# One core: both halves of one modulation vector summed on VectorE, several mixer steps handed to ScalarE and GpSimd, and one routing reorder

## The chip, the cores and the metric

One core of a Trainium2 chip. The metric is the device time of the program in microseconds (us); smaller is better. The kernel before has a median of 685.8 us over 3 runs (685.34 to 686.16). The trace that is read below is one further, profiled execution of it.

## The reference

A trunk of two layers over 256 tokens of width 1024, in float32. Every sub-layer is an RMS norm that is shifted, scaled and gated by vectors computed from the conditioning input c; a layer is a mixer (layer 0: sparse attention beside a spatial gating unit; layer 1: pooling) and then a mixture of 32 experts.

```python
cs = jax.nn.silu(c)
for i in range(DEPTH):
    mod = cs @ w_mod[i] + b_mod[i]                      # 1024 x 6144 per layer
    sh_m, sc_m, g_m, sh_f, sc_f, g_f = jnp.split(mod, 6, axis=-1)
    h = modulate(rmsnorm(x, norm_mix[i]), sh_m, sc_m)
    y = hybrid_ab(h, ...) if i % 2 == 0 else multiscale_pool(h, ...)
    x = x + g_m[:, None, :] * y
    h = modulate(rmsnorm(x, norm_ffn[i]), sh_f, sc_f)
    x = x + g_f[:, None, :] * hier_moe(h, ...)          # router, top 2 of 8 in the top group
return rmsnorm(x, norm_out)

# in hybrid_ab, layer 0:  h @ w_in gives q, kv, q_idx, k_idx, w_idx, u, v
#   attention over the 64 best keys of each query, distance penalty -slope * |i - j|, softmax
#   spatial gating: gelu(u) * (masked(w_s) @ layernorm(gelu(v)) + b_s)
#   concat([attention, gating]) @ w_o
```

## The kernel before, in words

All weights stream once from HBM (268 MB read), on SyncE's DMA queue. Large tiles of 2 MiB ("chunks") land in a few places: four ring slots, and the rooms `scratch` (ATT), `early_w`, `ARENA_A` and `ARENA_B`. The table `front` (L175 on) lists the chunks in their loading order, each with its place; SyncE issues a chunk once the chunk that held the place before has been used up (`slot_freed`), so a late user holds back a transfer and every one behind it in the queue. Later, in the expert loop, each pair of experts takes three transfers of 2 MiB (gate, up, down); the loads of the third pair wait for TensorE's gate matmuls of the first (`gate_next`, L346).

A modulation vector is named (layer, v): v = 0, 1, 2 are the mixer's shift, scale and gate, v = 3, 4, 5 those of the experts. The chunks m4a and m4b are the two halves of (0,4), m3a and m3b of (0,3), n1a and n1b of (1,1), n4a and n4b of (1,4). A half is multiplied by `cs` in one of two ways. TensorE does it in `vector` (L593, 16 matmuls written as 32 records). VectorE does it in `accumulate` (L1438, L1440): four steps over 128x1024, each adding one weight row per partition times a scalar; `reduce` (L614) then sums over partitions on TensorE. The lists `by_pe` and `by_dve` say which chunk goes which way, in order of use.

Each engine's order is written out by hand. In layer 0's mixer they are, around the change:

- VectorE: the index scores, `select(0)` and `select(1)` (best 64 keys), `|dist|` (L1532), `shift` and `divide` of the softmax, then `gelu_v` (polynomial L1514, L1515; after ScalarE's tanh L1539; layernorm statistics L1541 to L1543; GpSimd's power L520; L1546; scaling L1548), `keep_heads(0)` (L1581), the second half of (0,4), the gating unit's bias (L1592), the first half of (0,3), the polynomial of u, `keep_heads(1)`, two products (L1600, L1603, which raises `bT_ready`), the second half of (0,3), the second half of (1,4), and then both halves of (0,5) between the four parts of the residual (L1452, L1453).
- TensorE: scores (L727), the transposes of w_s (L743), q (L680), attention logits, v (L764), transposes of the probabilities (L789), first half of (0,4) (L593), `values(0)` (L797), half of u (L774), w_s times v (L821), second half of u (L774), `values(1)` (L797), the output projection (L841, 64 records), and in its middle the reductions of (0,4) and (0,3).
- ScalarE copies out of PSUM: half of the heads in `keep_heads` (L1217, to catT in `xn`), the tanh of v (L1222) and of u (L1226).
- Layer 0's routing on TensorE: logits (L876, L884), first half of (1,1), first half of (1,4) (both L593), the experts' totals (L902 on, which wait for VectorE's assignment L1667), second half of (1,1), the gather of tokens (L925), the first pair of experts (L960 gate, L972 up).

## Time and profile before

| | |
|---|---|
| median of 3 runs | 685.8 us |
| profiled execution | 686.04 us, of which span 684.3 us |
| TensorE matmul busy | 624.7 us (91%) |
| VectorE, ScalarE, GpSimd busy | 358.2, 179.4, 61.9 us (52, 26, 9%) |
| SyncE's DMA queue | 96.9% of 16 DMA engines' span, 268.22 MB |
| granted TensorE clock | 0.997 of full speed |

The page shows one execution. Busy shares are averages over unlike stages, so they do not say what ends a stage; the timeline of an engine and what ended its idle time do. Every start in a timeline counts from the start of the span. TensorE's float32 matmuls appear as two records each. A released wait is shown in square brackets behind the instruction.

### The profile page before, as it was taken

To read this page: it belongs to the slowest core of one execution; us is meant where nothing else is said; L and a number is where in the kernel's file an instruction comes from. 1 tells how busy PE (TensorE), PEld (TensorE's weight loads), DVE (VectorE), ACT (ScalarE), POOL (GpSimd) and SP (SyncE) were. 2 spreads that over 40 slices of the span, in tenths; PEclk is the share of its full clock that TensorE was granted. 3 is DMA by queue.
4 is the path that set the end of the run, shared out by engine and by line. 5 is a ranking of instruction groups with operands and counts; after the bars stand their busy time and mean duration, and the time that the engine had idled before them with its cause. 6 is when DMAs were issued, how large, how long until landed. Compare 5 with 4: busy or idle time off the path is not lost.

```text
span 684.3 us, 11444 instructions
## 1 busy us (share of the span) xinstructions
PE 624.7 (91%) x4226; PEld 376.5 (55%) x4226; DVE 358.2 (52%) x869; ACT 179.4 (26%) x370; POOL 61.9 (9%) x107
## 2 busy tenths in 40 slices
PE   2699999998999999999998989999999999999894
PEld 1487758446766555545554447676645554555442
DVE  2248988997554643344433464745344334433446
ACT  2123252013431222122311233343122212221213
POOL 5100508930000000000000000000000000000000
PEclk9999999999999999999999999999999999999998
DMA  8999987999899999999999999999999999999991
GB/s 330 355 394 394 370 278 264 404 416 416 352 413 419 420 421 422 420 422 422 422 423 421 409 398 411 422 419 420 421 421 421 422 422 421 422 421 422 422 396 72
DMA packets 51534, 269.63 MB, mean 394 GB/s; under 512 B 4112, under 2 KB 6224, under 8 KB 27440
## 3 DMA queue, kind: packets, MB, share of 16 engines
q1 hardware_dynamic: 50720, 268.22, 96.9%
q0 software_dynamic: 784, 1.01, 0.5%
q8 instruction: 19, 0.31, 0.2%
q14 instruction: 11, 0.09, 0.0%
HBM read 268.17 MB, written 1.05 MB: 393 GB/s over the span
## 4 chain that ended last, share of the span: by engine, by line
PE 69%; DMA 15%; DVE 10%; SPq 2%; issue 1%; ACT 1%; POOL 0%; DVEq 0%; POOLq 0%
PE bank L960 15%; PE bank L972 15%; PE bank L993 13%; PE bank L1019 8%; DMA ring<-in_w_gate 7%; DMA ring<-in_w_mod 4%; PE bank L680 4%; DMA early_w<-in_w_in 3%; DVE gates L1440 3%; PE bank L925 2%; PE bank L764 2%; DVE hT L1758 2%; PE bank L593 2%; PE bank L980 1%; PE bank L1076 1%
## 5 line engine op out<-in xcount | busy, mean ns | idle before, releaser
L960 PE MATMUL bank<-ring,arena 128*64 128x256 f32 x1024 | 116.8, 380 | 2.7 <-DMA ring<-in_w_gate 2.7
L972 PE MATMUL bank<-ring,arena 128*64 128x256 f32 x1024 | 117.2, 381 | 0.0
L960 PEld LDWEIGHTS bank<-ring,arena 128*64 128x64 f32 x1024 | 75.3, 137 | 51.0 <-issue 20.4
L972 PEld LDWEIGHTS bank<-ring,arena 128*64 128x64 f32 x1024 | 72.3, 137 | 41.1 <-issue 8.6
L1758 DVE SCALAR_TENSOR_TENSOR hT<-hT,bank 128x256 f32<-128x256 f32 x32 | 19.2, 601 | 136.6 <-PE bank L972 136.6
L1287 ACT CAST xn_parts<-arena 128x512 fp32r<-128x512 f32 x64 | 39.6, 619 | 106.8 <-DVE arena L1783 106.8
L1783 DVE SCALAR_TENSOR_TENSOR arena<-bank,hT,gates 128x512 f32<-128x512 f32 x64 | 48.0, 750 | 36.7 <-PE bank L993 35.4
L1019 PE MATMUL bank<-xn_parts,sel 128*128 128x512 f32 x256 | 67.0, 405 | 0.0
L993 PE MATMUL bank<-dn_w,hT 128*64 128x512 f32 x256 | 58.5, 598 | 1.1 <-ACT gates L1097 1.1
L1019 PEld LDWEIGHTS bank<-xn_parts,sel 128*128 128x128 f32 x256 | 45.7, 188 | 20.9 <-issue 12.4
L993 PE MATMUL bank<-xn,arena 128*64 128x512 f32 x112 | 51.1, 598 | 0.0
L993 PE MATMUL bank<-gates,arena 128*64 128x512 f32 x112 | 51.1, 598 | 0.0
L1753 DVE SCALAR_TENSOR_TENSOR hT<-hT,bank 128x256 f32<-128x256 f32 x32 | 13.5, 421 | 63.1 <-ACT hT L1274 63.0
L1788 DVE TENSOR_TENSOR xn_parts<-arena,xn_parts 128x512 fp32r<-128x512 f32 x64 | 44.0, 687 | 2.8
L1267 ACT COPY arena<-arena 128x512 f32 x64 | 39.9, 623 | 9.6 <-issue 6.1
L993 PEld LDWEIGHTS bank<-dn_w,hT 128*64 128x64 f32 x256 | 17.4, 136 | 30.9 <-issue 30.9
L593 PE MATMUL bank<-ring,cs 128*32 128x256 f32 x288 | 19.2, 414 | 16.2 <-DMA ring<-in_w_mod 16.2
L1440 DVE SCALAR_TENSOR_TENSOR gates<-ring,cs,gates 128x1024 f32<-128x1024 f32 x23 | 30.1, 1307 | 3.9 <-DMA ring<-in_w_mod 3.2
L980 PE MATMUL bank<-ident,hT 128*128 128x128 f32 x64 | 13.7, 295 | 19.3 <-DVE hT L1758 19.3
L1278 ACT COPY hT<-bank 128x256 f32<-128x256 f32 x16 | 6.0, 372 | 92.6 <-PE bank L980 92.6
L1278 ACT COPY arena<-bank 128x256 f32<-128x256 f32 x16 | 6.0, 373 | 88.1 <-PE bank L980 88.1
L993 PEld LDWEIGHTS bank<-xn,arena 128*64 128x64 f32 x112 | 14.2, 136 | 26.3 <-issue 26.3
(322 smaller groups left out, 761.8 us busy)
## 6 DMA issues: line engine op xcount, KB each, us to landing
ring<-in_w_gate SPq DMA_DIRECT2D x32, 2048.0 KB, 17.2
ring<-in_w_up SPq DMA_DIRECT2D x32, 2048.0 KB, 18.4
ring<-in_w_mod SPq DMA_DIRECT2D x20, 2048.0 KB, 18.4
dn_w<-in_w_down SPq DMA_DIRECT2D x16, 2048.0 KB, 18.2
xn<-in_w_down SPq DMA_DIRECT2D x14, 1024.0 KB, 16.9
gates<-in_w_down SPq DMA_DIRECT2D x14, 1024.0 KB, 19.2
ring<-in_w_in SPq DMA_DIRECT2D x2, 2048.0 KB, 23.8
dn_w<-in_w_mod SPq DMA_DIRECT2D x2, 2048.0 KB, 12.1
```

Of the source, the lines that this page charges most:

```text
L593: ins = pe.matmul(quadrant(vec, q), cs[:, 2, k:k + 1].to_broadcast([P, 32]), by_quadrant(w[:, kk, :], q, natural), start=not last and kk = ...
L680: ins = pe.matmul(bank[banks[m // 2]][:, (m % 2) * T:(m % 2 + 1) * T], w[:, k, m * P:(m + 1) * P], hT[:, k, :], start=(k == 0), stop=(k == ...
L960: ins = pe.matmul(bank[2][h * WIN:(h + 1) * WIN, 0:FE], xw[:, b, h, k, :], w[:, h, 0, k, :], start=(k == 0), stop=(k == KT - 1))
L972: ins = pe.matmul(bank[3][h * WIN:(h + 1) * WIN, 0:FE], xw[:, b, h, k, :], w[:, h, 1, k, :], start=(k == 0), stop=(k == KT - 1))
L993: ins = pe.matmul(bank[n][h * WIN:(h + 1) * WIN, :], actT[b][:, t, h * WIN:(h + 1) * WIN], w[h][:, t, n * HALF:(n + 1) * HALF], start=(t = ...
L1019: ins = pe.matmul(bank[4 + 2 * n + t][:, :], sel[:, b, t * P:(t + 1) * P], xn_parts[:, part, b, n * HALF:(n + 1) * HALF], start=(isinstanc ...
L1267: ins = act.copy(xw[:, b, h], xgT[:, :, bass.ds(start, WIN)])
L1287: act.copy(xn_parts[:, 0, b, at], y_s[:, b, at]).then_inc(e["y_hi"], 1)
L1440: ins = stt(acc, w, cs[:, 2, k:k + 1], acc, ALU.mult, ALU.add)
L1758: stt(act_s.rearrange("s t p -> s p t"), gl.rearrange("s (p t) -> s p t", t=FT), 0.5, bank[3][:, 0:FE].rearrange("s (p t) -> s p t", t=FT) ...
L1783: stt(y_s[:, b, at], bank[n][:, :], slot_gate[:, b:b + 1], gates[:, 2 * l + 1, at], ALU.mult, ALU.mult).then_inc(e["y_kept"], 1)
L1788: tt(xn_parts[:, 1, b, at], y_s[:, b, at], xn_parts[:, 0, b, at].bitcast(F32), ALU.subtract).then_inc(e["y_lo"], 1)
```

## The change

(0,4) moves whole to VectorE: its first half is summed right behind the last `divide`, ahead of `gelu_v`, and starts the sum (one tensor_scalar and three further steps); its second half is then four steps instead of one and three. TensorE's matmuls for m4a go. The reduction of (0,4) now starts the output projection, that of (0,3) stands ahead of the projection's second half.

VectorE gives up: `|dist|`, made by three GpSimd instructions over 128x512 early in the program; the zeroing of a corner of wsT, now a GpSimd memset; the first instruction of both gelu polynomials (0.044715 goes into the scale of ScalarE's square, the 1 into the one VectorE instruction that is left); both copies of `keep_heads`, now two 64-partition copies on ScalarE that both wait for the second half of the values; and the two scaling instructions of the layernorm of v, now two ScalarE instructions with a bias that VectorE prepares in one small one. The transposes of w_s go ahead of the scores on TensorE, into bank 1, and ScalarE copies them in two pieces ahead of the scores' relus. In layer 0's routing, both halves of (1,1) stand ahead of the totals, and the first half of (1,4) behind them.

ScalarE's order from the copy of the transposed probabilities to the one ahead of the squares: L1217, which writes catT (`xn`), is `keep_heads`; the instruction to dn_w of 128x1024 is a tanh. Before:

```order
L1209 COPY arena<-bank 128x512 x2
L1222 ACTIVATE dn_w<-dn_w 128x1024
L1217 COPY xn<-bank 64x4x128
L1105 COPY stage<-bank 128x256
L1191 COPY arena<-bank 128x512
L1192 ACTIVATE dn_w<-bank 128x512
L1212 COPY arena<-bank 128x2x256 x4
L1191 COPY arena<-bank 128x512
L1192 ACTIVATE dn_w<-bank 128x512
L1217 COPY xn<-bank 64x4x128
L1226 ACTIVATE dn_w<-dn_w 128x1024
```

And in the change:

```order
L1213 COPY arena<-bank 128x512 x2
L1228 ACTIVATE dn_w<-dn_w 128x1024
L1223 COPY xn<-bank 64x4x128 x2
L1106 COPY stage<-bank 128x256
L1232 ACTIVATE arena<-arena,stat 128x512 x2
L1195 COPY arena<-bank 128x512
L1196 ACTIVATE dn_w<-bank 128x512
L1216 COPY arena<-bank 128x2x256 x4
L1195 COPY arena<-bank 128x512
L1196 ACTIVATE dn_w<-bank 128x512
L1223 COPY xn<-bank 64x4x128 x2
L1237 ACTIVATE dn_w<-dn_w 128x1024
```

The heads' copies are pairs now, and the layernorm's scaling (L1232) stands ahead of the copies of u. The tanh of u still stands behind the heads' copies.

TensorE's order in layer 0's routing, from the logits to the gather (ARENA_A and ARENA_B are the `arena` rows, ATT is `dn_w`). Before:

```order
L876 MATMUL bank<-hT,wroute 64x256 x8
L884 MATMUL bank<-join,stage 128x40 x2
L593 MATMUL bank<-arena,cs 32x256 x16
L593 MATMUL bank<-dn_w,cs 32x256 x16
L902 MATMUL bank<-ones,rt 32x128
...
L913 MATMUL bank<-rt,ones 128x32
L593 MATMUL bank<-arena,cs 32x256 x16
L925 MATMUL bank<-sel,xn_parts 128x512 x32
```

And in the change:

```order
L879 MATMUL bank<-hT,wroute 64x256 x8
L887 MATMUL bank<-join,stage 128x40 x2
L597 MATMUL bank<-arena,cs 32x256 x32
L903 MATMUL bank<-ones,rt 32x128
...
L914 MATMUL bank<-rt,ones 128x32
L597 MATMUL bank<-dn_w,cs 32x256 x16
L926 MATMUL bank<-sel,xn_parts 128x512 x32
```

The 16 matmuls that read n4a (dn_w) moved from ahead of the totals to behind them.

```diff
-        by_dve = [m2a, m2b, m4b, m3a, m3b, n4b, m5a, m5b]
+        by_dve = [m2a, m2b, m4a, m4b, m3a, m3b, n4b, m5a, m5b]
...
             for t in range(TT):
                 done(pool.iota(dist[:, t, :], [[-1, T]], base=t * P, channel_multiplier=1,
                                allow_small_or_imprecise_dtypes=True))
+            pool.tensor_scalar(keep, dist, -1.0, 0.0, ALU.mult, ALU.max)
+            done(pool.tensor_scalar(dist, dist, 0.0, None, ALU.max))
+            done(pool.tensor_tensor(dist, dist, keep, ALU.add))
+            done(pool.memset(wsT[CHUNK:P, :, 0:CHUNK], 0.0))
...
+            pe.wait_ge(S["small_in"], 16 * SMALL)
+            pe.wait_ge(S["consts"], 2)
+            pe.wait_ge(S["col_turned"], 2)
+            for g in range(4):
+                ins = pe.transpose(bank[1][:, g * P:(g + 1) * P], ws_raw[:, g, :], ident[:])
+            ins.then_inc(S["ws_turned"], 1)
             pe.wait_ge(S["kiT_ready"], 1)
             pe.wait_ge(S["qi_kept"], 2)
...
             turn_p(1)
-            vector((0, 4), (0,))
             pe.wait_ge(S["v_kept"], 2)
...
             values(1)
-            pe.wait_ge(S["cat_act"], 2)
-            pe.wait_ge(S["cat_dve"], 2)
+            reduce((0, 4))
+            pe.wait_ge(S["cat_act"], 4)
             pe.wait_ge(S["u_kept"], 2)
...
-                    if half == 1 and (part, t) == (0, 1):
-                        reduce((0, 4)), reduce((0, 3))
+                    if half == 1 and (part, t) == (0, 0):
+                        reduce((0, 3))
...
                 if l == 0:
-                    vector((1, 1), (0,))
-                    pe.wait_ge(S["xn_part2"], 1)
-                    vector((1, 4), (0,))
+                    vector((1, 1))
...
                 if l == 0:
-                    vector((1, 1), (1,))
+                    vector((1, 4), (0,))
...
+            act.wait_ge(S["ws_turned"], 1)
+            act.wait_ge(S["consts"], 2)
+            turned_ws = bank[1][:, :].rearrange("p (g i) -> p g i", g=4)
+            act.copy(wsT[0:CHUNK], turned_ws[0:CHUNK])
+            act.copy(wsT[CHUNK:P, :, CHUNK:P], turned_ws[CHUNK:P, :, CHUNK:P]).then_inc(S["wsT_copied"], 1)
             for u in range(6):
                 act.wait_ge(S["score_done"], u + 1)
...
-                act.wait_ge(S["pv_done"], 2 * t + 1)
-                act.copy(catT[0:HD, 0:4, t * P:(t + 1) * P], bank[3][0:HD, :].rearrange("p (k q) -> p k q", k=4)
-                         ).then_inc(S["cat_act"], 1)
+                act.wait_ge(S["pv_done"], 2 * t + 2)
+                for b in range(2):
+                    at = slice(b * HD, (b + 1) * HD)
+                    act.copy(catT[at, 0:4, t * P:(t + 1) * P], bank[3 + b][at, :].rearrange("p (k q) -> p k q", k=4)
+                             ).then_inc(S["cat_act"], 1)
...
-            keep_heads(0), keep_column((1, 0)), keep_u(0), keep_p(2), keep_p(3), keep_p(4), keep_p(5), keep_u(1)
+            keep_heads(0), keep_column((1, 0))
+            act.wait_ge(S["ln_bias"], 1)
+            for t in range(TT):
+                ins = act.activation(vtk[:, t, :], vtk[:, t, :], ACT.Identity, scale=stat[:, 18 + t:19 + t], bias=stat[:, 16 + t:17 + t])
+            ins.then_inc(S["vln_ready"], 1)
+            keep_u(0), keep_p(2), keep_p(3), keep_p(4), keep_p(5), keep_u(1)
             keep_heads(1)
...
-                done(ts(sq, sq, GELU_A, 1.0, ALU.mult, ALU.add))
-                tt(sq, sq, v, ALU.mult).then_inc(after, 1)
+                stt(sq, sq, 1.0, v, ALU.add, ALU.mult).then_inc(after, 1)
...
+            accumulate((0, 4), 0)
             gelu_v()
-            keep_heads(0)
             accumulate((0, 4), 1)
...
             gelu_poly(flat(usq), flat(uT), S["u_poly"])
-            keep_heads(1)
             dve.wait_ge(S["u_tanh"], 1)
```

## Rows read from the trace of the kernel before

**Rows 1.** The page's slices of 17.1 us: GB/s of the transfers.
```profile
GB/s 330 355 394 394 370 278 264 404 416 416 352 413 419 420 421 422 420 422 422 422 423 421 409 398 411 422 419 420 421 421 421 422 422 421 422 421 422 422 396 72
```

**Rows 2.** Four microseconds: busy time (count) by engine, granted clock, DMA share, GB/s.
```profile
180.00:184.00 4.00, 4.00 (x42) 2.64 (x38) 0.71 (x3) 1.62 (x3) 0.00 (x0) 1.00 0.52 127
```

**Rows 3.** Timeline of SyncE's queue at the first gate load that waits: start, us, line, instruction.
```profile
181.57 0.38 SPq L346 DMA_DIRECT2D ring<-in_w_gate  x1
```

**Rows 4.** Timeline of VectorE in the mixer: start, us, line, operation, [idle before].
```profile
95.20 0.62 DVE L1575 TENSOR_SCALAR dn_w<-dn_w,asum 128x256 f32<-128x256 f32 x2
...
100.44 1.23 DVE L1539 SCALAR_TENSOR_TENSOR arena<-dn_w,arena 128x1024 f32<-128x1024 f32 x1 [1.12 <-ACT dn_w L1222]
...
104.63 0.52 DVE L1546 TENSOR_SCALAR stat<-stat 128x2 f32<-128x2 f32 x1 [0.83 <-POOL stat L520]
...
105.19 1.05 DVE L1548 TENSOR_SCALAR arena<-arena,rt,stat 128x512 f32<-128x512 f32 x2
...
113.61 5.33 DVE L1440 SCALAR_TENSOR_TENSOR gates<-ring,cs,gates 128x1024 f32<-128x1024 f32 x4
...
122.51 1.22 DVE L1600 SCALAR_TENSOR_TENSOR arena<-dn_w,arena 128x1024 f32<-128x1024 f32 x1
...
124.91 5.43 DVE L1440 SCALAR_TENSOR_TENSOR gates<-ring,cs,gates 128x1024 f32<-128x1024 f32 x4
...
131.04 0.75 DVE L1438 TENSOR_SCALAR arena<-ring,cs 128x1024 f32<-128x1024 f32 x1 [0.69 <-DMA ring<-in_w_mod]
...
152.52 0.69 DVE L1452 TENSOR_TENSOR hT<-bank,gates 128x512 f32<-128x512 f32 x1
```

**Rows 5.** Timeline of TensorE in the mixer, 97 to 134 us.
```profile
108.47 1.95 PE L821 MATMUL bank<-arena 128*128 128x128 f32 x16
...
111.13 7.07 PE L774 MATMUL bank<-hT,ring 128*128 128x256 f32 x32
...
118.04 3.60 PE L797 MATMUL bank<-arena 128*128 128x512 f32 x8
...
122.47 11.83 PE L841 MATMUL bank<-early_w,xn 128*128 128x512 f32 x27 [0.83 <-issue]
```

**Rows 6.** Timeline of TensorE in layer 0's routing, 159 to 165 us.
```profile
159.11 1.93 PE L593 MATMUL bank<-arena,cs 128*32 128x256 f32 x32
...
162.95 1.93 PE L593 MATMUL bank<-dn_w,cs 128*32 128x256 f32 x32 [1.91 <-issue]
...
164.67 0.38 PE L902 MATMUL bank<-ones,rt 128*32 128x128 f32 x2
```

**Rows 7.** Timeline of VectorE in layer 0's routing.
```profile
162.86 0.23 DVE L1667 TENSOR_TENSOR rt<-rt 128x64 f32<-128x64 f32 x1
```

**Rows 8.** Timeline of VectorE in layer 1's routing.
```profile
437.14 0.23 DVE L1667 TENSOR_TENSOR rt<-rt 128x64 f32<-128x64 f32 x1
```

**Rows 9.** Timeline of TensorE in layer 1's routing.
```profile
437.43 0.41 PE L902 MATMUL bank<-ones,rt 128*32 128x128 f32 x2 [0.93 <-DVE rt L1667]
```

**Rows 10.** The page's groups: ScalarE from SBUF, 128x512.
```profile
L1267 ACT COPY arena<-arena 128x512 f32 x64 | 39.9, 623 | 9.6 <-issue 6.1
```

**Rows 11.** Timeline of ScalarE, 119 to 123 us.
```profile
119.96 0.58 ACT L1217 COPY xn<-bank 64x512 f32<-64x512 f32 x1 [0.63 <-PE bank L797]
...
121.42 1.06 ACT L1226 ACTIVATE dn_w<-dn_w 128x1024 f32<-128x1024 f32 x1 [0.88 <-DVE dn_w L1515]
```

**Rows 12.** Timeline of TensorE at the scores, 54 to 61 us.
```profile
54.88 2.03 PE L727 MATMUL bank<-arena 64*128 64x128 f32 x24 [0.72 <-issue]
...
59.77 0.66 PE L743 MATMUL bank<-ident,arena 128*128 128x128 f32 x4
```

**Rows 13.** Timeline of ScalarE at the scores.
```profile
56.04 1.09 ACT L1162 ACTIVATE arena<-bank 128x512 f32<-128x512 f32 x2 [1.26 <-PE bank L727]
```

**Rows 14.** Timeline of GpSimd as it builds the pooling band: two like instructions.
```profile
105.20 0.31 POOL L526 TENSOR_SCALAR_AFFINE_SELECT band<-band 128x144 f32<-128x144 f32 x1
...
108.35 1.18 POOL L526 TENSOR_SCALAR_AFFINE_SELECT band<-band 128x144 f32<-128x144 f32 x1
```

More of the change, by code:

```diff
@@ L186, in trunk @@
         place = {key: n for n, key in enumerate(plan)}
[L187 to L189 removed]
+        by_dve = [m2a, m2b, m4a, m4b, m3a, m3b, n4b, m5a, m5b]
+        by_pe = [("mod", 0), ("mod", 1), ("mod", 2), ("mod", 3), ("in", "kv"), ("in", "qi"), n0a, ("in", "q"), n0b, ("in", "v"), ("in", "u"),
+                 ("out", 0), ("out", 1), n1a, n1b, n4a] + [m for m, slot in middle]
         assert sorted(by_dve + by_pe, key=str) == sorted(plan, key=str)
@@ L1163, in _ @@
                                ).then_inc(S["score_relu"], 1)
-            act.wait_ge(S["ws_turned"], 1)
-            act.copy(flat(wsT), bank[7][:, :]).then_inc(S["wsT_copied"], 1)
             keep_gate((0, 2))
@@ L1430, in accumulate @@
                     done(ts(acc, rows[:, :], ident[:, r:r + 1], None, ALU.mult))
-                elif part == 0:
+                elif part == 0 and vec != (0, 4):
                     dve.wait_ge(S["bias_kept"], ((0, 3), (0, 5)).index(vec) + 1)
@@ L1436, in accumulate @@
                     w = mod_at(place[key])[:, kk, :]
-                    if kk == 0 and part == 1 and halves(vec)[0] in by_pe:
+                    if kk == 0 and (part == 1 and halves(vec)[0] in by_pe or part == 0 and vec == (0, 4)):
                         ins = ts(acc, w, cs[:, 2, k:k + 1], None, ALU.mult)
@@ L1525, in select @@
                 done(ts(keep[:, t, 0:(t + 1) * P], s, TAKEN, FAR, ALU.not_equal, ALU.mult))
+            dve.wait_ge(S["consts"], 2)
             select(0)
             select(1)
-            dve.wait_ge(S["wsT_copied"], 1)
-            dve.memset(wsT[CHUNK:P, :, 0:CHUNK], 0.0).then_inc(S["wsT_ready"], 1)
-            dve.wait_ge(S["consts"], 2)
-            done(stt(flat(dist), flat(dist), -1.0, flat(dist), ALU.mult, ALU.max))
             def gelu_v():
```

32 lines of the change are left out of this document (9 added, 23 removed).

## The prediction

> **What bounds the kernel now.** I read the page's slices first. From the eighth slice on (120 us) the transfers run near 420 GB/s almost without a break, through both expert loops [rows 1]. The loops therefore finish when their bytes are in, and a gain can only come from time in which the DMA engines had nothing to do. The reader finds two low places: slices six and seven (86 to 120 us, 278 and 264 GB/s) and slice eleven (171 to 188 us, 352) [rows 1]. The bytes of the first are made good by a later wait: all that may be loaded ahead of the experts is in by 180 us. The second place counts. A closer view of 180 to 184 us gives a DMA share of 0.52 and 127 GB/s [rows 2]: the ring and the down rooms are full, and the next load goes out only at 181.57 us, when TensorE has done the gate matmuls of the first expert pair [rows 3]. From there the stream doesn't break, so **the program's end moves by what that issue at 181.57 us moves**, as long as the queue runs dry before it. It had 1.9 us of nothing in these four (4 x 0.48), so it may run dry some 1 us later than now without a loss.
>
> So the question is the chain up to 181.57 us. In the timeline of VectorE from 95 to 153 us [rows 4] the bracketed idle times are few: it waits for ScalarE, for GpSimd's power and, at 131.04 us, 0.69 us for a transfer; from there to the last part of the residual at 152.52 us it waits for nothing. TensorE is ahead of it there: its output projection starts at 122.47 us after 0.83 us of waiting [rows 5], and no VectorE row behind 131 us waits for it. In the routing it is TensorE that is late: it idles 1.91 us in front of the matmuls that read n4a, a transfer still on its way, and reaches the totals at 164.67 us [rows 6], though VectorE's assignment, at 162.86 us, was long there [rows 7]. In layer 1, where nothing of the sort stands in front, the same two instructions are 437.14 and 437.43 us [rows 8, 9]: 0.29 us apart where layer 0 has 1.81.
>
> **The change, part by part.** I follow the chain from the end of the last divide, 95.20 + 0.62 = 95.8 us [rows 4].
>
> First half of (0,4) on VectorE: one tensor_scalar (0.75) and three steps; four steps take 5.33 us, one 1.33 [rows 4]. Sum 0.75 + 4.0 = 4.75, until 100.6 us. Of this 1.5 us was idle time before the polynomial anyway; TensorE's matmuls that go (1.93 us, as [rows 6]) gain nothing, since TensorE will wait for the layernorm below.
>
> gelu of v: the polynomial is now one two-input instruction, 1.2 us as at 122.51 [rows 4], until 101.8. ScalarE's tanh 1.06 [rows 11], until 102.9. From the product to the instruction behind GpSimd's power: 104.63 - 100.44 = 4.2, so 107.1. That instruction and its wait 0.56 (105.19 - 104.63), and the new two-element one for the bias: between next to nothing and the 0.52 of its neighbour of the same width [rows 4]; I take 0.25. Ready at 107.9 us.
>
> The scaling on ScalarE: VectorE took 1.05 for two [rows 4]; ScalarE's nearest form is 623 ns [rows 10], so 1.25. Bounds 1.05 and 1.45 with hand-over. TensorE's w_s times v starts at 109.2 instead of 108.47 [rows 5], +0.7. The move also frees VectorE for 1.05 us, which the wait further down shows to be worth nothing. The Trainium skill's page "ScalarE: Activation LUTs" (section "Rules for kernel authors") speaks against it: multiply and add belong on VectorE. By the rows the step loses 0.2 us, and by that rule the sum without it would be 685.4.
>
> From w_s times v to the second half of u is 111.13 - 108.47 = 2.66, to the values 6.91, and these take 3.60 [rows 5]: 111.9, 118.8 and 122.4 us. ScalarE's copies of the transposed probabilities stand behind its scaling but are done in time, half a microsecond before TensorE wants the banks.
>
> **The new wait.** Both head copies are ScalarE's now, and both wait for the second half of the values. The tanh of u stands behind them. Two copies of 0.58 [rows 11]: 123.6; tanh until 124.6. VectorE meanwhile has finished the second half of (0,4) at 113.2 (107.9 + 5.3), the gating bias (1.6, the four instructions that end at 113.61 now), the first half of (0,3) (5.3) and u's polynomial (1.2) at 121.4 us; it idles 3.2 us. So what VectorE is spared here, both head copies and the shorter polynomial, turns into a wait. Its two products take 124.91 - 122.51 = 2.4 [rows 4]: the second half of (0,3) starts at 127.0 rather than 124.91, **+2.1**. Here 0.7 comes back, as the transfer that was waited for at 131.04 us [rows 4] has landed by then. m3b goes out when the second half of (0,4) is done, at 113.2 where it is now 113.61 - 1.6 = 112.0, so n4b, two chunks behind it, lands by 131.04 + 1.2 = 132.2; VectorE comes at 132.3. Everything up to 152.52 us is back to back, and moves by **+1.3**. TensorE's projection moves by 1.1 and stays ahead.
>
> The routing: both halves of (1,1) landed long before, and take 159.11 + 1.3 + 3.8 = 164.2 us [rows 6]; the assignment comes at 164.2, the totals 0.3 behind it. That is **-1.5** (1.81 - 0.29) [rows 6, 7]. Behind them the first half of (1,4), 1.93 us, replaces an equal one, and its transfer had landed at 162.95 (now within 1.3 us of that). The down load that waits for n4a's use goes out some 4 us later, behind four transfers of 1 and 2 MiB that are queued and not yet in: nothing.
>
> The front: the transposes of w_s (0.66) fit in a gap of 0.72 us [rows 12], and two ScalarE copies (0.6 and 0.4 at most) end by 55.8, before the relu at 56.04 [rows 13]: they can start when TensorE's 54.88 - 0.72 = 54.2 has become 54.8. I take 0; uncovered, it is 0.66 + 1.2 = 1.9 us, since VectorE's scores start from that relu. `|dist|` and the memset, taken off VectorE, only bring it sooner to its wait for TensorE's attention logits, which come behind q without a gap on TensorE: 0. GpSimd's four new instructions stand early, in front of its long wait for a chunk: 0.
>
> Sum: +1.3 - 1.5 = -0.2 us. Against the profiled execution 686.04 gives 685.8; the median lies 0.24 below it, so **685.6 us**.
>
> **The shared port.** The same GpSimd instruction on the band takes 0.31 us at 105.20, and 1.18 at 108.35 beside VectorE's two-input steps [rows 14], while four such steps take VectorE 5.33 us at 113.61 and 5.43 at 124.91, both beside GpSimd [rows 4], about their 1.3 each. So GpSimd pays, and in the change the band only starts 2.5 us later: 0. The Trainium skill's page "SBUF — State Buffer" (section "SBUF: two separate sides") says that the port pair which the two share is an exclusive lock, held for the whole instruction by whoever starts first. By that rule VectorE can lose too, up to one GpSimd instruction each time it comes second.
>
> **The rivals.**
> *The mixer comes out even* (0.18). If the second half of u starts no later than now, or VectorE's steps are shorter beside an idle TensorE, the +1.3 goes and -1.5 stays: 684.3 us. For it: TensorE drops 1.93 us of work before the values. Against: the tanh of u behind 122.4 us follows from rows 5 and 11 alone.
> *The w_s work ahead of the scores is not covered* (0.10): slower. Place: ScalarE before the relu at 56.04 us. The margin is 0.2 us [rows 12, 13]; from there on every microsecond passes through the scores, q and v, where TensorE has no gap. At its full 1.9 us: 687.5 us. Against it: all its inputs are long there.
> *The routing gives nothing* (0.07), as the totals then wait for something else (n1b, or a bank): 685.6 + 1.5 = 687.1 us.
> *GpSimd holds the port* (0.05): VectorE's two small instructions at 107 us stand on the chain, now beside the band's first ones; each waits for one of them, 0.35 as the 0.52 of rows 4 suggests: 0.7 in all, 686.3 us. This is how the lock of the State Buffer page of the Trainium skill would show here.
>
> **How the numbers follow.** My forecast has 0.60. A measurement can tell about 0.2% (1.4 us) from no change, so the bounds are 684.4 and 687.2. The forecast lies inside but for 0.02 on each side; of the first rival 0.18 counts as faster; of the second 0.09 and of the third 0.04 as slower (687.1 is near the bound). Faster 0.20, same 0.65, slower 0.15. The range takes in the first rival and most of the second: 684.2 to 687.3.
>
> **What would show it.** Right: VectorE idle 3 us before its product of u, the tanh of u starting behind a second head copy at 123.5; no idle time at the (1,4) half; the totals 0.3 us behind the assignment; the gate load at 181.3. Wrong: a relu later than 56.2, a tanh of u before 122.5, or a gate load more than 1 us away from 181.57.

## The result, and the profile after

The changed kernel takes **688.41 us** (median of 20 runs, 685.74 to 692.01); the kernel before, run beside it, 686.2 (20 runs). The ratio is 1.0033, 95% interval 1.0022 to 1.0045: slower by 2.2 us, 1.1 us above the forecast's range. The forecast was 685.6. Three executions among all that are told of below (756 us of `e1`, 1325 and 1669 us of the kernel before) were in a far slower state and count in no ratio and no average.

The profiled execution took 691.05 us, its span is 688.9 and its mean granted clock 0.984; before it was 684.3 and 0.997. It is among the longest of the 20, so it shows the loss enlarged.

VectorE's timeline of the changed kernel, 79 to 154 us, beside [rows 4] (columns as there):

```profile
79.64 0.88 DVE L1565 SCALAR_TENSOR_TENSOR arena<-arena,bank 128x128 f32<-128x128 f32 x4 [1.64 <-PE bank L731]
...
95.12 0.75 DVE L1449 TENSOR_SCALAR gates<-ring,cs 128x1024 f32<-128x1024 f32 x1
95.91 3.92 DVE L1451 SCALAR_TENSOR_TENSOR gates<-ring,cs,gates 128x1024 f32<-128x1024 f32 x3
99.87 1.23 DVE L1525 SCALAR_TENSOR_TENSOR dn_w<-dn_w,arena 128x1024 f32<-128x1024 f32 x1
...
106.97 0.16 DVE L1555 SCALAR_TENSOR_TENSOR stat<-rt,stat 128x2 f32<-128x2 f32 x1
...
124.40 1.23 DVE L1598 SCALAR_TENSOR_TENSOR arena<-dn_w,arena 128x1024 f32<-128x1024 f32 x1 [3.31 <-ACT dn_w L1237]
...
126.80 5.44 DVE L1451 SCALAR_TENSOR_TENSOR gates<-ring,cs,gates 128x1024 f32<-128x1024 f32 x4
132.27 0.77 DVE L1449 TENSOR_SCALAR arena<-ring,cs 128x1024 f32<-128x1024 f32 x1
...
153.80 0.69 DVE L1463 TENSOR_TENSOR hT<-bank,gates 128x512 f32<-128x512 f32 x1
```

The mixer went as foretold: 3.31 us of idle time ahead of u's product, none at the half of (1,4), the last residual at 153.80 against 152.52. ScalarE, from 102 to 124 us, beside [rows 11]:

```profile
107.16 1.52 ACT L1232 ACTIVATE arena<-arena,stat 128x512 f32<-128x512 f32 x2 [3.51 <-DVE stat L1555]
...
122.10 1.18 ACT L1223 COPY xn<-bank 64x512 f32<-64x512 f32 x2 [2.35 <-PE bank L803]
123.31 1.06 ACT L1237 ACTIVATE dn_w<-dn_w 128x1024 f32<-128x1024 f32 x1
```

What was not foretold is on TensorE, behind the mixer. Its timeline in layer 0's routing, changed kernel:

```profile
152.24 1.16 PE L658 MATMUL bank<-ident,x_res 128*128 128x128 f32 x8 [0.40 <-DVE x_res L1464]
153.91 0.83 PE L869 MATMUL bank<-wroute,ab 128*128 128x40 f32 x6 [0.51 <-DVE ab L1417]
155.27 1.97 PE L658 MATMUL bank<-ident,x_res 128*128 128x128 f32 x8 [0.53 <-DVE x_res L1464]
157.04 2.19 PE L869 MATMUL bank<-wroute,ab 128*128 128x40 f32 x10
159.16 3.40 PE L879 MATMUL bank<-hT,wroute 128*64 128x256 f32 x16
163.03 0.64 PE L887 MATMUL bank<-join,stage 128*128 128x40 f32 x4 [0.47 <-ACT stage L1259]
163.60 3.66 PE L597 MATMUL bank<-arena,cs 128*32 128x256 f32 x64
167.63 0.41 PE L903 MATMUL bank<-ones,rt 128*32 128x128 f32 x2 [0.37 <-DVE rt L1665]
```

The same stretch before:

```profile
151.21 1.04 PE L654 MATMUL bank<-ident,x_res 128*128 128x128 f32 x8
152.63 0.83 PE L866 MATMUL bank<-wroute,ab 128*128 128x40 f32 x6 [0.38 <-DVE ab L1406]
153.99 1.16 PE L654 MATMUL bank<-ident,x_res 128*128 128x128 f32 x8 [0.53 <-DVE x_res L1453]
154.99 1.21 PE L866 MATMUL bank<-wroute,ab 128*128 128x40 f32 x10
156.12 1.95 PE L876 MATMUL bank<-hT,wroute 128*64 128x256 f32 x16
```

Transposes, fold and logits take 1.97, 2.19 and 3.40 us for 1.16, 1.21 and 1.95. The table of stretches says why (busy time and count by engine, then the granted clock, DMA share, GB/s), changed kernel:

```profile
154.00:156.00 2.00, 1.47 (x10) 1.35 (x11) 1.35 (x3) 0.72 (x2) 0.00 (x0) 0.83 0.99 412
156.00:158.00 2.00, 2.00 (x12) 2.00 (x10) 1.31 (x4) 1.94 (x5) 0.72 (x1) 0.50 1.02 410
158.00:160.00 2.00, 2.00 (x10) 1.61 (x12) 1.21 (x4) 0.66 (x1) 0.00 (x0) 0.50 1.02 410
160.00:162.00 2.00, 2.00 (x12) 1.18 (x10) 0.79 (x1) 0.00 (x0) 0.00 (x0) 0.50 1.06 432
```

The granted clock is 0.50, the lower of the two levels (1.2 GHz for 2.4), from about 156 to 162 us, in instructions with ScalarE, VectorE and then the gate load behind them. Before, the same stretch has 1.00. It falls again in layer 1's routing, 440 to 450 us (changed kernel, four stretches):

```profile
436.00:440.00 4.00, 3.21 (x44) 1.09 (x36) 3.55 (x16) 0.00 (x0) 0.00 (x0) 1.00 1.02 420
440.00:444.00 4.00, 3.84 (x20) 3.05 (x21) 3.35 (x14) 1.37 (x4) 0.00 (x0) 0.75 1.02 424
444.00:448.00 4.00, 4.00 (x8) 2.17 (x7) 3.73 (x20) 1.17 (x2) 0.00 (x0) 0.50 1.01 422
448.00:452.00 4.00, 4.00 (x16) 3.81 (x16) 2.27 (x8) 1.55 (x2) 0.00 (x0) 0.89 1.01 416
```

The gate load of [rows 3], and the dry queue around it, which before had 0.52 over four microseconds [rows 2]:

```profile
184.55 0.38 SPq L346 DMA_DIRECT2D ring<-in_w_gate  x1
```

```profile
182.00:184.00 2.00, 2.00 (x20) 1.12 (x18) 1.24 (x8) 1.42 (x4) 0.00 (x0) 1.00 0.03 12
184.00:186.00 2.00, 2.00 (x22) 1.34 (x20) 0.42 (x1) 0.71 (x2) 0.00 (x0) 1.00 0.30 41
```

**Where the 4.6 us between the two spans are.** Four marks cut the program: VectorE's first `shift` (80.25 us before, 79.64 now), the last residual part (152.52, 153.80), the gate load (181.57, 184.55), the end (684.3, 688.9).

| stretch | before | changed | difference |
|---|---|---|---|
| start to first shift | 80.25 | 79.64 | -0.61 |
| first shift to last residual part | 72.27 | 74.16 | +1.89 |
| last residual part to gate load | 29.05 | 30.75 | +1.70 |
| gate load to end | 502.73 | 504.35 | +1.62 |

The first stretch varies by itself: from the first matmul to the shift it is 68.07 us before and 66.82 to 68.16 in the experiments. The second and the third are what the experiments take apart; the fourth is read from the traces further down.

### The profile page after: what moved, and what is told of

Read it like the earlier page. It is cut to its first block, busy times and chain, and to the rows that moved or that the text cites. A ratio compares the mean times of both kernels' runs of the same rounds, so it can differ in the third digit from the quotient of the medians.

```text
span 688.9 us, 11387 instructions
## 1 busy us (share of the span) xinstructions
PE 629.7 (91%) x4194; PEld 379.3 (55%) x4194; DVE 359.0 (52%) x866; ACT 182.5 (26%) x375; POOL 67.2 (10%) x111
## 4 chain that ended last, share of the span: by engine, by line
PE 70%; DVE 15%; DMA 8%; SPq 4%; issue 1%; ACT 1%; POOL 0%; DVEq 0%; POOLq 0%; ACTq 0%
PE bank L961 16%; PE bank L973 16%; PE bank L994 14%; PE bank L1020 8%; DMA ring<-in_w_mod 5%; DVE gates L1451 4%; DMA ring<-in_w_gate 4%; PE bank L926 2%; DVE hT L1756 2%; PE bank L684 2%; SPq L343 2%; PE bank L981 2%; PE bank L780 1%; PE bank L1077 1%; SPq L333 1%
## 5 line engine op out<-in xcount | busy, mean ns | idle before, releaser
L1451 DVE SCALAR_TENSOR_TENSOR gates<-ring,cs,gates 128x1024 f32<-128x1024 f32 x27 | 35.0, 1297 | 4.3 <-DMA ring<-in_w_mod 3.5
L472 POOL TENSOR_TENSOR stat<-stat,mhalf 128x2 f32<-128x2 f32 x4 | 2.8, 706 | 285.9 <-DVE stat L1371 285.9
```

The lines of the kernel that those rows point to most:

```text
L1451: ins = stt(acc, w, cs[:, 2, k:k + 1], acc, ALU.mult, ALU.add)
```

## The experiments

Eighteen kernels were run, each timed in turn with the kernel before (its medians lay between 685.83 and 686.35). "Clean" below means that the profile's granted clock is 1.00 throughout the stretch. In the kernels with a filler, that matmul computes nothing that is read.

My theory after the first look was that TensorE's short waits in the routing bring the fall, and that the fall is what is lost. The rivals: the mixer's own work is dearer than I had summed; or falls come with the changed mixer whatever the waits are.

**The parts apart.** `e1_routing_only` is the kernel before with the routing's part:

```diff
-("out", 0), ("out", 1), n1a, n4a, n1b]
+("out", 0), ("out", 1), n1a, n1b, n4a]
-                    vector((1, 1), (0,))
-                    pe.wait_ge(S["xn_part2"], 1)
-                    vector((1, 4), (0,))
+                    vector((1, 1))
                 else:
                     vector((1, 5))
...
                 if l == 0:
-                    vector((1, 1), (1,))
+                    vector((1, 4), (0,))
```

> The kernel before with the routing's part of the change alone: both halves of (1,1) ahead of the totals, the first half of (1,4) behind them. Theory A (the work moves as forecast, and what is on top of it is TensorE's clock, which falls to 1.2 GHz in the routing in some executions): the first gate load that waits moves from 181.57 to about 180.0 us, 1.5 us less than before in an execution at full clock, ratio about 0.998. Theory B (the routing reorder gives nothing or costs, the mixer's part is as forecast): no gain, ratio 1.000 to 1.002, totals no sooner than 164.6 us.

`e2_mixer_only` is the changed kernel with that diff reversed.

> The changed kernel with the routing in its old order, so the mixer's part of the change alone. Theory A: +1.3 us in an execution at full clock (gate load near 182.9 us), and on top 3 us in those in which the clock falls in layer 0's routing. If the mixer's part is what makes the clock fall (TensorE waits longer for VectorE behind the output projection), the mean granted clock is below that of the kernel before and the ratio 1.003 to 1.006. If the routing's part makes it fall, the ratio is 1.002 and the clock stays at 0.997.

Measured: `e1` 685.91 us, ratio 0.9993 (0.9978 to 1.0009); `e2` 689.88, 1.0060 (1.0037 to 1.0082). On the changed mixer the medians of the two orders are 1.5 us apart, as they should be, but `e2` has seven runs only and the intervals overlap. On the kernel before the reorder is worth nothing in the median, and its fastest run is 682.95. Its profile shows the totals 0.28 us behind the assignment, as meant, and then TensorE at half clock behind them, at the half of (1,4) that stands before the gather (`e1`, TensorE; 1.93 us in [rows 6]):

```profile
162.09 0.41 PE L900 MATMUL bank<-ones,rt 128*32 128x128 f32 x2 [0.37 <-DVE rt L1665]
...
164.55 3.58 PE L593 MATMUL bank<-dn_w,cs 128*32 128x256 f32 x32
168.06 8.21 PE L923 MATMUL bank<-sel,xn_parts 128*128 128x512 f32 x32
```

`e2` fell at 156 to 163 us like the changed kernel, logits 3.40 us. It tells what the old order does in such a fall: the last residual part to the totals took 169.38 - 155.55 = 13.83 us, the same 13.83 as in the changed kernel (167.63 - 153.80), while clean it is 12.15 in the old order and 10.63 in the new (`e1`, 162.09 - 151.46). So the wait of TensorE for n4a [rows 6] was a cushion: a fall at the logits costs 1.7 us in the old order and 3.2 in the new, and with such a fall both orders take the same 30.75 us up to the gate load.

**The wait for the tanh, and real work in the gap.** `e3_tanh_first` and `e4_fill_gap`, both from the changed kernel:

```diff
-            keep_heads(1)
             act.wait_ge(S["u_poly"], 1)
             act.activation(flat(usq), flat(usq), ACT.Tanh, scale=GELU_C).then_inc(S["u_tanh"], 1)
+            keep_heads(1)
```
```diff
                 if l == 0:
+                    vector((1, 1), (0,))
                     turn_raw(l, (0,))
...
-                    vector((1, 1))
+                    vector((1, 1), (1,))
```

> The changed kernel with ScalarE's tanh of u ahead of its two copies of the second heads. The wait of 3.3 us on VectorE before its product of u goes; then the transfer of n4b ends the wait at the (1,4) half, near 131.3 us instead of 132.27, so the chain is only about 1 us shorter: ratio 0.9985 of the changed kernel at equal clock, 1.001 to 1.002 of the kernel before with falls of the clock, 0.999 without. If VectorE's wait was worth its whole 3.3 us, 0.995 of the changed kernel.

> The changed kernel with the first half of (1,1), 32 records of matmul, ahead of the first transposes of the new residual, where TensorE sits idle for 1.4 us in all. It delays nothing by the trace (the second transposes wait for VectorE at 155.2 us anyway). Theory A (the clock falls because TensorE is idle or only transposes there): the clock stays at full speed through layer 0's routing, the logits matmuls take 1.95 us and not 3.40, mean clock at or above 0.990, median 2 us below the changed kernel's, ratio about 1.000. Rival (the fall has nothing to do with this place): the clock falls as often and the ratio stays at 1.003.

Measured: `e3` 687.32 us, 1.0016 (1.0003 to 1.0028), clean in its routing (last residual part to gate load 27.54 us). `e4` 690.22, 1.0067 (1.0044 to 1.0089): no fall at 156 us, but TensorE then idles 2.09 us before the totals, and falls behind them, with 0.71 and 0.50 at 164 to 172 us. The work only moved the gap, to a place where it was longer.

**Fillers, and the half back.** `e5_fill_before_turns`, `e6_fill_routing` and `e7_routing_filled` (this one from `e1`) put a `fill` ahead of TensorE's waits; `e8_first_half_back` undoes one part of the mixer:

```diff
+    for i in range(n if l == 0 else 0):                         # fill(b, n)
+        pe.matmul(bank[b][:, :], ident[:], rows[:, 0:HALF], start=True, stop=True)
...
+    free_banks(pe, (1, 1))
+    fill(1, 2)                                                  # e5: here alone; e6, e7: at five waits
     turn_raw(l, (0,))
```
```diff
-    by_dve = [m2a, m2b, m4a, m4b, m3a, m3b, n4b, m5a, m5b]      # e8
+    by_dve = [m2a, m2b, m4b, m3a, m3b, n4b, m5a, m5b]           # m4a behind ("in", "v") in by_pe
+    vector((0, 4), (0,))                                        # TensorE, behind turn_p(1)
-    accumulate((0, 4), 0)                                       # VectorE
```

> The changed kernel with two added TensorE matmuls of 128x512 into a bank nobody reads (0.42 us of work) between the out projection and the first transposes of layer 0's routing, where the changed kernel's profile has 0.40 us of idle TensorE and the earlier versions whose clock held (the kernel before, the tanh-first version) had none. They add work that computes nothing. Theory A (TensorE's waits at the end of the out projection and in the transposes cost it the clock of the routing): the profile's clock at 156 to 162 stays 1.00, the logits take 1.95 us, the gate load is issued about 181.4, and the median falls from 688.4 to 686.0 to 687.0. Theory B (the fall follows from the whole mixer's thinner TensorE work or comes by chance, so a filler of 0.4 us is beside the point): clock 0.5 again in some part of 155 to 172, median 688 to 689.

> The changed kernel with fillers of the same kind at every wait of TensorE in layer 0's routing: two before the first transposes, two before the first fold, two before the second transposes, two before the join, one before the totals. Theory A: clock 1.00 from 150 to 168 and fewer runs with a mean clock under 0.988, median 686.0 to 687.0, the same as with the first filler or 0.3 us later where a filler overruns its wait. Theory B: mean clock 0.990 as before, median 688 to 689. Whatever is left over 685.9 after the clock holds is the cost of the change's own work: the mixer's +1.3 less the routing's 1.5 predicts nothing left, 685.7.

> The kernel before with the routing's part of the change alone, and the same fillers. Without fillers it stood at 685.9, with the totals 1.5 us earlier but TensorE at half clock from 164 to 168, behind the totals. Theory A: with the waits filled that fall goes too, the 1.5 us reach the gate load (180.0), and the median is 684.3 to 685.0, faster than the kernel before. Theory B: mean clock 0.991 to 0.992 and 685.5 to 686.5.

> The changed kernel with the first half of (0,4) back on TensorE at its old place behind the turned probabilities; everything else of the change is kept. VectorE gets back 4.75 us at 95.9, its GELU chain starts at 95.9 and not 100.6. Theory A: the mixer is no longer late, u's product comes at 123 or earlier, the last residual at 151.5 to 152.5, there is no 0.40 us wait before the routing's transposes, no fall of the clock at 156, and the median is 684.5 to 686.0. Theory B (the mixer's moved parts other than this half, or the routing's order, cost the clock): residual as early, but the clock falls in the routing all the same and the median is 686.5 or more.

Measured: 687.88 us (1.0025, 1.0014 to 1.0037), 692.99 (1.0099, 1.0082 to 1.0115), 690.38 (1.0066, 1.0051 to 1.0081) and 687.16 (1.0021, 1.0004 to 1.0038). The fillers were mis-sized: two took 1.88 us where 0.42 was meant, for two float32 matmuls of 128x512 are four records, and at five places they put 4.8 and 5.8 us on the chain (last residual part to gate load 32.30 and 33.30 for 27.53). `e6` and `e7` therefore answer nothing about the median. They and `e5` do have clean profiles from 150 to 172 us. In `e8` the chain is what was hoped for, but its median isn't: its profiled execution, clean, took 684.43 us, yet its runs reach 691.32, the lower the mean clock the longer.

**Fillers of the right size.** `e9_half_back_filled` (from `e8`), `e10_changed_filled`, `e12_routing_filled_once` (from `e1`), and `e11_before_with_wait`, which was to make the kernel before wait:

```diff
+    pe.matmul(bank[1][:, 0:C], ident[:], rows[:, 0:C], start=True, stop=True)   # ahead of turn_raw(l, (0,)); e9: C = 128, e10: 256
+    pe.matmul(bank[2][:, 0:128], ident[:], rows[:, 0:128], start=True, stop=True)   # e12: ahead of the wait for asg_ready
+    if gate == 0 and n == 2:                                                        # e11: residual, VectorE
+        done(tt(y[:, 0:256], bank[b][:, 0:256], gates[:, gate, HALF:HALF + 256], ALU.mult))
```

> The changed kernel with (0,4)'s first half back on TensorE (as in the last run) and one short filler of 0.24 us (128x128, computes nothing) before the first transposes of layer 0's routing, where that run's profile had TensorE waiting 0.19 us. Theory A (a wait of TensorE at just this point brings the fall of its clock into the transposes and logits; of the versions so far those with the wait, 0.40, 0.40 and 0.19 us, gained 0.30 to 0.44 us for each 0.001 of mean clock that a run lost, those without it 0.00 to 0.15): the profile is clean at 150 to 158, the spread over runs shrinks to about 684.3 to 686.5, the median is 684.5 to 685.5 against 687.16 without the filler. Theory B (the wait has nothing to do with it): 687.2 plus up to 0.1, with the same spread of 684.4 to 691.

> The changed kernel with one filler of 0.47 us (128x256) in the 0.40 us wait before the first transposes; the earlier filler was 1.88 us, four times what was meant, and made the chain itself later. Theory A: full clock in 155 to 160, logits 1.95 us, gate load at about 181.6, median 686.3 to 687.0, highest run under 689. Theory B: median 688.4, runs up to 692.

> The kernel before, with a repeated product of 128x256 on VectorE (0.4 us, it computes the same values twice) ahead of the third of the four residuals, so that the first x_ready comes 0.4 us later and TensorE has to wait 0.4 us before its first transposes; nothing else is changed. By the chain alone it costs 0.4 us: 686.2. Theory A: falls of the clock come into the routing here too, median 687.2 to 688.5, runs up to 691, and time against clock as steep as in the changed kernel. Theory B: 686.2 with the spread of the kernel before.

> The kernel before with the routing's order of the change, and one filler of 0.24 us in the 0.37 us wait before the routing's totals, where the profile of that order without a filler had the clock fall right behind the totals. Theory A: the fall behind the totals goes, the 1.5 us arrive, median 684.3 to 685.0 against 685.9. Theory B: 685.9 as without it.

Measured: `e9` 685.63 us (0.9999, 0.9977 to 1.0020), `e10` 687.60 (1.0024, 1.0002 to 1.0047), `e11` 686.24 (1.0005, 0.9989 to 1.0022), `e12` **684.64** (0.9981, 0.9965 to 0.9996). `e12` is the one clear gain, 1.3 us under `e1` by a matmul of 0.49 us in a wait of 0.37. Its TensorE has no fall there, and the half of (1,4) takes 1.93 again:

```profile
161.64 0.49 PE L898 MATMUL bank<-rows,ident 128*128 128x128 f32 x2
162.09 0.41 PE L902 MATMUL bank<-ones,rt 128*32 128x128 f32 x2
...
164.55 1.93 PE L593 MATMUL bank<-dn_w,cs 128*32 128x256 f32 x32
166.95 5.26 PE L925 MATMUL bank<-sel,xn_parts 128*128 128x512 f32 x20 [0.47 <-DVE sel L1693]
```

`e9` stands 1.5 us under `e8`, but with runs up to 688.76; `e10` came out between its two theories, with runs up to 691.77, and speaks for neither.

`e11` did not test the wait: its transposes (150.92 us) show none, for TensorE came just as late as VectorE. It shows another thing: the 0.4 us on VectorE came back at the wait for n4a, which shrank from 1.91 us [rows 6] to 1.33.

**Taking the mixer's part down step by step.** `e13_half_back_totals_filled` (`e8`), `e15_tanh_first_totals_filled` (`e3`) and `e16_changed_totals_filled` (the changed kernel) each get `e12`'s one filler. `e14_copies_back_too` is `e13` with the scaling and half of the head copies on VectorE again; `e17_both_filled_best` is `e14`, and `e18_changed_both_filled` is `e16`, with `e10`'s filler as well.

```diff
-    for t in range(TT):                                          # e14, ScalarE
-        ins = act.activation(vtk[:, t, :], vtk[:, t, :], ACT.Identity, scale=..., bias=...)
+    for t in range(TT):                                          # VectorE, in gelu_v
+        ins = ts(vtk[:, t, :], vtk[:, t, :], rt[:, 680 + 2 * t:681 + 2 * t], stat[:, 18 + t:19 + t], ALU.subtract, ALU.mult)
+    keep_heads(0)                                                # VectorE, behind gelu_v
+    keep_heads(1)                                                # VectorE, behind u's polynomial
```

> The changed kernel with (0,4)'s first half back on TensorE, and one filler of 0.24 us (computes nothing) in the 0.37 us wait before layer 0's totals. Without it this mixer stood at 687.16. Theory A' (the wait that matters is the one before the totals, as it did for the kernel before with the new routing: 685.88 to 684.64): median 684.5 to 686.0. Theory C (the changed mixer itself brings the falls, wherever the routing waits): 686.5 to 687.2.

> As the last, and the layernorm's scaling and the head copies are back on VectorE, so that of the mixer's part there remain: w_s turned early, its copies and the distance on ScalarE and GpSimd, and the GELU polynomial in one VectorE instruction. ScalarE is then free for the tanh of u as soon as the polynomial is there, and the 3.31 us wait of VectorE before the product of u should shrink to under 1 us: product at 121.5 or earlier, last residual at 151.0 or earlier, gate load at 178.7. By the chain 684.0 to 684.6, at or below the kernel before with the new routing and the filler (684.64). Rival: the moved w_s work alone brings the loss, 685.5 or more.

> The changed kernel with the tanh of u ahead of the second head copies (687.32 before) and the filler of 0.24 us before the totals. Theory A': 686.0 to 686.6. Theory C: 687.0 to 687.4.

> The changed kernel, whole, with nothing but the filler of 0.24 us before layer 0's totals. Theory A': the falls behind the totals go, 687.0 to 687.6 against 688.41; what is left over the kernel before is the mixer. Theory C: 688.0 to 688.6. Its profile is also a second one of the changed mixer with its 0.40 us wait before the transposes: if the fall at 156 is bound to that wait it is there again, if it comes by chance it may not be.

> The fourteenth kernel (new routing order, w_s turned early, fused GELU polynomial; first half of (0,4) on TensorE, copies and scaling on VectorE, filler of 0.24 us before the totals) with a second filler of 0.47 us (128x256, computes nothing) in the 0.47 us wait of TensorE before the first transposes. That kernel stood at 684.71, with 4 of its 12 runs between 687.5 and 690.7 at mean clocks of 0.984 to 0.989. If those 4 are falls of the clock that begin at this wait, they go: highest run under 687, mean 684.6, median 684.3 to 684.8. If they have another cause: a third of the runs again above 687, mean 685.9.

> The changed kernel with both fillers, 0.47 us before the first transposes and 0.24 us before the totals (alone they gave 687.60 and 688.78 against 688.41). If the fall at 155 to 163 needs the wait before the transposes, and the totals' filler is worth the 1.0 to 1.2 us that it gave three other versions once the earlier fall is out of the way: 686.3 to 686.8, logits at 1.95 us. If the changed mixer brings falls whatever the waits: 687.5 to 688.5 with runs up to 692.

Measured: `e13` 686.14 us (0.9992, 0.9980 to 1.0003), `e14` 684.71 (0.9989, 0.9968 to 1.0010), `e15` 686.36 (0.9998, 0.9986 to 1.0010), `e16` 688.78 (1.0028, 1.0014 to 1.0041), `e17` 684.61 (0.9981, 0.9963 to 0.9998), `e18` 687.21 (1.0017, 1.0002 to 1.0033).

The medians with the totals' filler are 1.3, 1.0 and 1.0 us lower (`e1` to `e12`, `e8` to `e13`, `e3` to `e15`), but not on the changed kernel (688.41 to 688.78). Only the first of the three had a fall behind the totals in its profile for the filler to remove; `e8` and `e3` were clean there without it, and the filler ahead of the transposes gave `e8` as much (`e9`). So that it is this place that matters is not shown for them. On the changed kernel `e16`'s profile shows why the filler could not help: the fall had begun earlier, at the same instructions as in the changed kernel, with the same durations (`e16`, TensorE):

```profile
152.97 1.16 PE L658 MATMUL bank<-ident,x_res 128*128 128x128 f32 x8 [0.41 <-DVE x_res L1466]
154.64 0.83 PE L869 MATMUL bank<-wroute,ab 128*128 128x40 f32 x6 [0.51 <-DVE ab L1419]
156.00 1.97 PE L658 MATMUL bank<-ident,x_res 128*128 128x128 f32 x8 [0.53 <-DVE x_res L1466]
157.76 2.19 PE L869 MATMUL bank<-wroute,ab 128*128 128x40 f32 x10
159.89 3.27 PE L879 MATMUL bank<-hT,wroute 128*64 128x256 f32 x16
```

It is not bound to the 0.40 us wait before the transposes, though: `e15`, without one, and `e17`, with it filled, fell a little later (`e17`, TensorE; the transposes are whole, the logits not):

```profile
151.06 1.04 PE L658 MATMUL bank<-ident,x_res 128*128 128x128 f32 x8
152.50 0.83 PE L872 MATMUL bank<-wroute,ab 128*128 128x40 f32 x6 [0.40 <-DVE ab L1418]
153.86 1.16 PE L658 MATMUL bank<-ident,x_res 128*128 128x128 f32 x8 [0.53 <-DVE x_res L1465]
154.86 1.68 PE L872 MATMUL bank<-wroute,ab 128*128 128x40 f32 x10
156.46 3.09 PE L882 MATMUL bank<-hT,wroute 128*64 128x256 f32 x16
```

My theory that the wait at just this point makes the fall has fallen with these two. `e18`, clean at the logits, came out between its two theories, with runs up to 690.25. `e17` still had one run in 12 above 687 us where `e14` had four.

**What the marks say.** From the profiles, in us:

| kernel | first shift to last residual part | last residual part to gate load | clock at the logits |
|---|---|---|---|
| before | 72.27 | 29.05 (old order) | clean |
| changed, `e2`, `e16` | 74.16, 74.16, 74.16 | 30.75, 30.75, 30.62 | half |
| changed mixer, `e10`, `e18` | 74.16, 74.15 | 27.52, 27.54 | clean |
| tanh first, `e3` and `e15` | 73.52, 73.43 | 27.54, 29.17 | clean, half in part |
| half back, `e8`, `e9`, `e13` | 72.90, 72.90, 72.89 | 27.53, 27.52, 27.53 | clean |
| and copies back, `e14`, `e17` | 72.72, 72.29 | 27.52, 29.16 | clean, half in part |
| mixer as before, `e1`, `e12` | 72.15, 72.11 | 28.67 (fall behind the totals), 27.54 | clean |

At a held clock the second stretch repeats within 0.03 us for the new order. The first does within 0.1 for the changed mixer and within 0.2 for the old one; where VectorE waits for the transfer of n4b it follows that transfer (a wait of 1.35 us in `e14` and 0.96 in `e17`, the same mixer). The change's routing is worth 29.05 - 27.53 = 1.52 us. Its mixer costs 74.16 - 72.27 = 1.89; of this (0,4)'s half on VectorE is 1.26 (74.16 to 72.90), and the tanh behind the head copies 0.64 to 0.73, two amounts that overlap. The earlier tanh brought the second half of (0,3) 2.20 us forward (44.96 us behind the shift in `e3`, 47.16 in the changed kernel), but most of it went into a wait of 1.81 us for n4b. A fall at the logits costs 30.75 - 27.53 = 3.22 us.

## Why the prediction was wrong, point by point

**The view of the end held as long as the clock did.** From the gate load to the end it is 502.5 to 503.8 us in 16 of the 18 experiments, 502.73 before; a gate load at 179.40 us (`e8`) gives a span of 682.3, one at 186.30 (`e2`) 689.2. The exceptions are 504.10 (`e12`), 504.55 (`e16`) and the changed kernel's 504.35. The last two share something that the forecast had ruled out ("From there the stream doesn't break"): a hole in the stream in layer 1. The totals there, the next gate load that waits, and the table of stretches behind it, changed kernel:

```profile
440.16 0.41 PE L903 MATMUL bank<-ones,rt 128*32 128x128 f32 x2 [0.94 <-DVE rt L1665]
```
```profile
459.36 0.38 SPq L346 DMA_DIRECT2D ring<-in_w_gate  x1
```
```profile
460.00:464.00 4.00, 3.22 (x30) 1.86 (x28) 0.80 (x2) 0.00 (x0) 0.00 (x0) 1.00 0.96 330
```

Before (totals at 437.43 [rows 9]):

```profile
454.32 0.38 SPq L346 DMA_DIRECT2D ring<-in_w_gate  x1
```
```profile
460.00:464.00 4.00, 4.00 (x40) 2.69 (x38) 0.42 (x1) 1.26 (x3) 0.00 (x0) 1.00 1.03 428
```

From the totals to that load it is 19.20 us for 16.89, +2.31, through the fall at 440 to 450. Then the stream moved 330 GB/s from 460 to 464 us, in `e16` 236, and 403 or more in every other profile. By the GB/s of the two stretches from 456 to 464 (395 and 330, for 422 and 428) the missing bytes are some 1.2 of the 1.62 us, an estimate; the rest is open, and so is `e12`, which has no hole. `e3` and `e5` fell here as well, but for less (17.72 and 17.62 us from totals to load), made no hole, and have 502.88 and 502.62.

**The mixer's +1.3 was too small: 1.89.** In absolute times it looked exact (153.80 against a forecast of 153.8), but only because this execution reached its first shift 0.61 us earlier. Counted from there, the second half of (0,3) came at 47.16 us against 44.66 before, +2.5 for the +2.1 of the sum (whose 2.1 less 0.7 is 1.4, put as 1.3). The term that was mis-sized is the scaling on ScalarE. I took 1.25 us with next to no hand-over; it took 1.52, and w_s times v began at 108.83, 1.70 us behind the bias (106.97 + 0.16), where I had 1.3. The rest of the chain (tanh 1.06, 4.20 from product to power, two copies 1.18, 0.66 coming back at n4b) was right within 0.1 us.

**Routing -1.5: right, when the clock holds** (1.52). The totals stood 0.28 us behind the assignment.

**The front, GpSimd and the port: right.** The relu moved from 56.04 to 54.90 us. GpSimd's first band instruction took 0.32 us again, and VectorE's two-element instruction at 106.97 waited for nothing. As in [rows 14] it was GpSimd that was slowed (its second band instruction took 1.17 us, before 0.37), while four of VectorE's steps took 5.24 to 5.44.

**The sum: wrong at its first assumption, that TensorE keeps its clock.** With both terms as measured it is +1.89 - 1.52 = +0.37, not -0.2: by that alone 686.2 in the forecast's terms, or 686.6 beside the 686.2 that the kernel before took this time; no measurable change. What the sum left out at nothing is a fall of the clock: each row was taken from one profile in which TensorE never lost it before the last microseconds, and no rival let it fall. In the profile of the changed kernel the fall at the logits costs 3.22 us and the one in layer 1 most of another 1.62.

The timed runs point the same way. Over a whole run the mean granted clock is 0.9904 for the changed kernel (20 runs) and 0.9920 for the kernel before (141 runs, those beside the experiments). Where it is 0.995 or more, they average 686.8 (4 runs) and 685.9 us (34); where it is under 0.9895, 690.2 (7 of 20) and 687.5 (29 of 141). So of the 2.2 us between 0.4 (by the traces) and 0.9 (by four runs) stands at a held clock, and the rest goes with falls. Each costs more, since the reorder took away the wait that used to absorb 1.5 us of a fall. Whether there are more of them is not settled by 7 of 20 against 29 of 141. Of the three signs of a wrong forecast that I had listed one came true: a gate load more than 1 us away from 181.57.

**Shown, and not shown.** Shown: the place and price of the fall, the cushion in the old order (by one profile of each kernel), and the cost of the mixer and of its larger pieces at a held clock. Not shown: why the clock falls, and whether the changed mixer brings falls about. Of the 15 profiles with all or part of its mixer (its own among them) five fell at the logits, of the five with the old mixer none; one profile of each kernel is too few to call this a cause. A rival that no experiment parts from it is what the execution did before: all five had also lost the clock at 20 to 40 us, before the first matmuls that the change moved (the w_s transposes, at 52.85 us). Of the five profiles of such a mixer that kept the clock there none fell at the logits, though four of these (all but `e8`) had a filler in the routing. Nor is a wait of TensorE shown to be the cause: it was there without a fall (`e8`, 0.19 us; `e14`, 0.47) and absent with one (`e15`). The Trainium skill's page "TensorE: Matmul & The Clock Gate" (section "A second HAM failure mode: psum-queue depth-cycling") says of one bf16 kernel that frequent short idle times between groups of matmuls make the clock go back and forth; the waits of 0.40, 0.51 and 0.53 us ahead of the fall agree with it, but the kernel before has 0.38 and 0.53 there without one.

**The best version.** `e12` (reorder, one filler, mixer as before) and `e17` (reorder, two fillers, and of the mixer's part only w_s, |dist| and the shorter polynomials) stand at 684.64 and 684.61 us, ratio 0.9981 each with intervals that end just under 1 (0.9996 and 0.9998): 1.3 and 1.4 us faster than the kernel before, 3.8 faster than the changed one. They are the best two of eighteen, so a part of that may be luck. `e12` has the smaller spread, 683.26 to 685.80.

## What to carry to other kernels

A chain of short TensorE instructions between waits is priced twice: at the clock of the profile, and once more at half of it, with a chance; a change that is worth 1.5 us by removing a wait may also remove what absorbed such a fall. Count a stage's cost from a mark inside the same execution, for here a start 0.61 us earlier hid that a term was too small. When a duty goes to another engine, follow what stands behind it there: the head copies that VectorE gave up bought it only idle time, and the two that ScalarE makes now put 1.2 us ahead of a tanh that VectorE waits for.

## What was not expected of the hardware

- TensorE's granted clock fell to 0.50 in the middle of a program whose TensorE is 91% busy, behind waits of 0.40, 0.51 and 0.53 us, and came back some 7 us later. The same instructions were slowed to the same durations in three kernels (1.97, 2.19 and 3.27 to 3.40 us for 1.16, 1.21 and 1.95).
- In 12 of the 20 profiles the clock fell at 20 to 40 us as well; in ten of them the first matmuls of the kv projection took 7.33 us for 5.65.
- The fillers took more than was meant: two float32 matmuls of 128x512 1.88 us, one of 128x256 0.59 and one of 128x128 0.38 to 0.49. A filler is to be measured before it is placed.
- A fall in layer 1 can cost bytes: with TensorE later at its first gate matmuls there, the stream dropped to 330 and 236 GB/s over four microseconds in two profiles, for 428 before.
